# First projection of a two-layer diffusion backbone by halves of the features, and expert weights in longer DMA rows

## What is computed

```
def modulation(cond, w_mod, b_mod):
    m = jax.nn.silu(cond) @ w_mod + b_mod
    return jnp.split(m[..., None, :], 6, axis=-1)

def modulate(x, shift, scale):
    return x * (1.0 + scale) + shift
...
    z = h @ w_in                       # even layer: 1024 -> 1184, h = modulate(x, shift, scale)
...
def moe(h, router_w, router_bias, w_gate, w_up, w_down):
    ...
    hid = jax.nn.silu(jnp.einsum("nd,edf->nef", x, w_gate)) * jnp.einsum("nd,edf->nef", x, w_up)
    y = jnp.einsum("nef,efd->nd", hid * gates[:, :, None].astype(hid.dtype), w_down)
...
        xp = layer_norm(ALPHA * xp + mp[2] * op, ln_g[l, 0], ln_b[l, 0])
        hp = modulate(xp, mp[3], mp[4])
        fp = moe(hp, router_w, router_bias, exp_w_gate[l], exp_w_up[l], exp_w_down[l])
        xp = layer_norm(ALPHA * xp + mp[5] * fp, ln_g[l, 1], ln_b[l, 1])
```

## Time and profile before

| | us |
|---|---|
| median of 3 runs | 795.42 |
| the profiled execution, whole | 793.16 |
| its span, first to last instruction | 791.4 |
| PE busy | 734.0 (93%) |
| DVE, ACT, POOL busy | 237.2, 157.5, 73.1 |
| data moved | 287.40 MB, mean 363 GB/s |
| DMA packets | 67906, of them under 8 KB 51988 |

### The profile page before, as it was taken

The page is one execution under the profiler, slowest core; times in us unless marked ns, Lnnn a source line. Parts: engine busy times, 40 slices in busy tenths (PEclk is TensorE's granted clock), DMA queues, the critical chain, the costliest instruction groups (busy, mean ns, idle before and its releaser), DMA issues.

```text
span 791.4 us, 9516 instructions
## 1 busy us (share of the span) xinstructions
PE 734.0 (93%) x3745; PEld 345.0 (44%) x3745; DVE 237.2 (30%) x551; ACT 157.5 (20%) x408; POOL 73.1 (9%) x126
## 2 busy tenths in 40 slices
PE   4699899897999999998799999998999999998896
PEld 1345444455444443443234554454544434442432
DVE  0003544455310010100436228484501001000255
ACT  0201321325011110120103132343211101110201
POOL 0000000000200001102200110000200002101020
PEclk9899899997999999999999999999899999999998
DMA  8999999915499999999999999963299999999993
GB/s 324 397 322 410 410 409 419 417 77 213 186 420 416 417 422 415 421 416 416 419 399 379 409 410 418 397 239 144 98 420 416 422 418 416 422 416 419 415 409 116
DMA packets 67906, 287.40 MB, mean 363 GB/s; under 512 B 6636, under 2 KB 12268, under 8 KB 51988
## 3 DMA queue, kind: packets, MB, share of 16 engines
q1 hardware_dynamic: 63828, 275.54, 86.6%
q10 hardware_dynamic: 2880, 7.03, 2.2%
q0 software_dynamic: 1152, 4.19, 1.3%
HBM read 278.93 MB, written 7.82 MB: 362 GB/s over the span
## 4 chain that ended last, share of the span: by engine, by line
PE 51%; SPq 31%; DMA 9%; DVE 5%; ACT 2%; issue 2%; POOL 0%; DVEq 0%; ACTq 0%
PE bank L1171 14%; SPq L638 12%; PE bank L1207 7%; PE bank L987 7%; SPq L633 6%; DMA ring<-in_exp_w_up 6%; PE bank L838 5%; SPq L634 4%; PE bank L1138 4%; DMA ring<-in_w_mod 3%; PE bank L725 3%; SPq L598 3%; SPq L602 2%; PE bank L966 1%; PE bank L943 1%
## 5 line engine op out<-in xcount | busy, mean ns | idle before, releaser
L1171 PE MATMUL bank<-ring,arena 128*64 128x512 f32 x1024 | 226.2, 597 | 7.8 <-DMA ring<-in_exp_w_up 7.8
L1171 PEld LDWEIGHTS bank<-ring,arena 128*64 128x64 f32 x1024 | 73.5, 138 | 156.5 <-issue 151.5
L1207 PE MATMUL bank<-ring,arena 128*64 128x512 f32 x512 | 113.8, 595 | 6.8 <-DMA ring<-in_exp_w_down 5.7
L1787 DVE TENSOR_TENSOR arena<-bank,arena 128x256 f32<-128x256 f32 x32 | 13.6, 425 | 218.8 <-ACT arena L1993 218.5
L1207 PEld LDWEIGHTS bank<-ring,arena 128*64 128x64 f32 x512 | 36.3, 137 | 73.9 <-issue 66.0
L1138 PE MATMUL bank<-arena 128*128 128x128 f32 x512 | 63.5, 279 | 0.0
L1138 PEld LDWEIGHTS bank<-arena 128*128 128x128 f32 x512 | 61.1, 196 | 1.2 <-issue 0.7
L725 PE MATMUL bank<-ring,cwin 128*32 128x512 f32 x384 | 50.4, 665 | 11.0 <-DMA ring<-in_w_mod 10.4
L1884 ACT ACTIVATE arena<-bank 128x512 f32<-128x512 f32 (+5 forms) x65 | 34.8, 559 | 116.2 <-PE bank L838 32.6
L1993 ACT ACTIVATE arena<-bank 128x256 f32<-128x256 f32 x32 | 12.3, 383 | 219.2 <-PE bank L1171 219.2
L1803 DVE COPY arena<-bank 128x512 f32<-128x512 f32 x14 | 9.7, 691 | 121.9 <-PE bank L1207 121.9
(11 more groups left out here) (200 smaller groups left out, 652.7 us busy)
## 6 DMA issues: line engine op xcount, KB each, us to landing
ring<-in_exp_w_gate SPq DMA_DIRECT2D x62, 1024.0 KB, 20.6
ring<-in_exp_w_up SPq DMA_DIRECT2D x62, 1024.0 KB, 20.3
ring<-in_exp_w_down SPq DMA_DIRECT2D x60, 1024.0 KB, 22.5
ring<-in_w_mod SPq DMA_DIRECT2D x24, 2048.0 KB, 21.5
expert_rows<-arena ACTq DMA_DIRECT2D x12, 512.0 KB, 7.8
ring<-in_w_out_ab SPq DMA_DIRECT2D x2, 2048.0 KB, 23.6
ring<-in_exp_w_down SPq DMA_DIRECT2D x8, 512.0 KB, 15.0
ring<-in_w_in_c SPq DMA_DIRECT2D x2, 2048.0 KB, 18.0
```

What stands on the lines that cost most here:

```text
L1171: mm = nc.tensor.matmul(pb(key)[SLOTS * hf:SLOTS * (hf + 1), :], xeT[b][:, k * P + SLOTS * a:k * P + SLOTS * (a + 1)], w[:, :, k % 4, hf * ...
L1207: mm = nc.tensor.matmul(pb(key)[SLOTS * a:SLOTS * (a + 1), :], hp[:, c:c + SLOTS], w[:, a, kf % 2, hf * HALF:(hf + 1) * HALF], start=(kf = ...
```

## The change

1. `plan_blocks` and `load_block`: modulation pieces 0 to 3 become four blocks `top`, each with all eight k of 512 columns (rows of 2 KB where they had 4 KB). Pieces 0 and 2 hold the first half of the features of shift and scale, 1 and 3 the second. The three `win` blocks become ranges of k (0 to 2, 3 to 5, 6 and 7) with whole rows of 1184 columns. The order is top 0, top 2, win 0, top 1, top 3, win 1, win 2; x is loaded behind the second block.
2. On PE, `top_chunks(h)`, `even_rows_turned(h)` and `project_even(part)` take the place of `modulation(0, 0)`, `modulated(0, 0)` and `project(0)`: half of the columns, x of that half turned, three steps of k of the projection, then the other half. The six (column range, group) outputs stand open in banks 0 to 5 together. ACT and DVE make `hT` by halves.
3. `w_down` is laid out `(p k) c`: partition p holds four consecutive rows, so a block's two rows are one piece of 8 KB. Hidden value f then has to stand at partition f // 4, so `gate_up` reads the columns of gate and up with a step of four elements (16 bytes), in all pairs.
4. In pairs 1 to 6, where the two slots of an expert lie closer than 8 apart (`whole`), one slot holds the whole gate matrix and the other the whole up matrix, in pieces of 16 KB per partition. Each slot is loaded by two DMAs, partitions 0 to 63 and 64 to 127. `gate_up` waits for both slots before its first matmul and reads both at once. The first expert's two slots are released at the second matmul of the second expert, the second expert's first slot behind the gather (chunks 4 and 5), its other as before.

```
-    order = [("mod", 0, c) for c in MOD_PIECES[0]] + [("win", 0, b) for b in range(3)]
+    order = [("top", 0, 0), ("top", 0, 2), ("win", 0, 0), ("top", 0, 1), ("top", 0, 3), ("win", 0, 1), ("win", 0, 2)]
...
+        def whole(n):
+
+            l = order[n][1]
+            return exp_n[l] + 6 <= n < exp_n[l] + 6 * (N_PAIR - 1) and abs(slot[n] - slot[n + 1]) < RING - 2
+
+        def whole_pair(n):
+
+            a, b = slot[n], slot[n + 1]
+            both = ring.rearrange("p (s c) -> p s c", c=BLK)[:, min(a, b):max(a, b) + 1:abs(a - b), :]
+            return both.rearrange("p w (k m r) -> p w k r m", k=KD, r=4)
...
-        w_down = i_["exp_w_down"].rearrange("l e (k p) c -> (l e) p k c", p=P)
+        w_down = i_["exp_w_down"].rearrange("l e (p k) c -> (l e) p k c", p=P)
...
+                    elif t < 4 and whole(n + t - t % 2):
+                        m = n + t - t % 2
+                        src = (w_up if (t % 2 == 1) == (slot[m] < slot[m + 1]) else w_gate)[e + t // 2]
+                        for r in (0, 64):
+                            sp.dma_start(block_ap(n + t)[r:r + 64, :], src[r:r + 64, :]).then_inc(got(n + t)[0], 16)
...
-                        pe.wait_ge(*got(n + k // 4, i))
+                        if not whole(n):
+                            pe.wait_ge(*got(n + k // 4, i))
+                        elif k == 0:
+                            for m in range(2):
+                                pe.wait_ge(*got(n + m, i))
...
-                    w = block_ap(n + k // 4).rearrange("p (w k f) -> p w k f", w=2, k=4)
+                    if whole(n):
+                        w = whole_pair(n)[:, :, k]
+                    else:
+                        w = block_ap(n + k // 4).rearrange("p (w k m r) -> p w k r m", w=2, k=4, r=4)[:, :, k % 4]
...
-                                              w[:, :, k % 4, hf * 256:(hf + 1) * 256],
+                                              w[:, :, 2 * hf:2 * hf + 2, :],
...
+                        elif (k, hf) == (0, 1) and a == 1 and whole(n - 2):
+                            mm.then_inc(*release(n - 2))
...
-                    modulation(0, 0)
-                    pe.wait_ge(*saved(("mod", 0, 0)))
-                    mod_columns(0, 0)
-                modulated(l, 0)
-                if l == 0:
-                    project(0)
+                    top_chunks(0)
+                    even_rows_turned(0)
+                    project_even(0)
+                    top_chunks(1, index[("win", 0, 0)])
+                    even_rows_turned(1)
+                    project_even(1)
+                    project_even(2)
```

More of the change, by code:

```diff
@@ L211, in plan_turns @@
     t = Turns()
-    t.use(("mod", 0, 0), 7)
     t.use(("lnT",), 5)
-    t.use(("modT", 0, 0), 6)
+    for h in range(2):
+        t.use(("top", h), 7)
+        t.use(("topT", h), 6)
+        for g in range(G):
+            t.use(("hT", 0, 0, g, h), 6 + g if h else 2 * g)
     for l in range(DEPTH):
         for s in range(2):
-            for g in range(G):
-                for q in range(2):
-                    t.use(("hT", l, s, g, q), 2 * g + q)
+            if (l, s) != (0, 0):
+                for g in range(G):
+                    for q in range(2):
+                        t.use(("hT", l, s, g, q), 2 * g + q)
             if s == 0:
@@ L748, in modulation, with top_chunks @@
                                  start=False, stop=True, skip_group_check=True).then_inc(*fill(key))
+            def top_chunks(h, used=None):
+                key = ("top", h)
+                room(pe, key)
+                out = pb(key)
+                for c in (h, 2 + h):
+                    n = index[("top", 0, c)]
+                    pe.wait_ge(*got(n))
+                    w = block_ap(n).rearrange("p (k c) -> p k c", k=KD)
+                    for k in range(KD):
+                        j = k % 4
+                        mm = nc.tensor.matmul(out[32 * j:32 * j + 32, :], cwin[:, k, 24 - 2 * c:56 - 2 * c], w[:, k, :],
+                                              start=(c == h and k < 4), stop=False, skip_group_check=True)
+                        if (c, k) == (h, 0) and used is not None:
+                            mm.then_inc(*release(used))
+                    mm.then_inc(*release(n))
+                bias = tri[0:DEPTH * N_MOD, 0:1].to_broadcast([DEPTH * N_MOD, 32]) if h else \
+                    cst(C_BIAS, 32, DEPTH * N_MOD)
+                nc.tensor.matmul(out[0:32, :], bias, rows[0:DEPTH * N_MOD, :],
+                                 start=False, stop=True, skip_group_check=True).then_inc(*fill(key))
+                pe.wait_ge(*saved(key))
+                turn_rows(("topT", h), mods[0], C_SEL, 8)
             def turn_rows(key, src, c0, n):
@@ L824, in project_odd, with even_rows_turned @@
+            def even_rows_turned(h):
+                pe.wait_ge(s_x, 32)
+                for g in range(G):
+                    rows_turned(0, 0, g, h)
             def project_odd():
@@ L1176, in gate_up @@
                             mm.then_inc(*release(used))
-                        elif (k, hf) == (4, 0):
+                        elif (k, hf) == (0, 1) and a == 1 and whole(n - 2):
+                            mm.then_inc(*release(n - 2))
+                        elif (k, hf) == (4, 0) and not whole(n):
                             mm.then_inc(*release(n))
@@ L1230, in pair @@
                 room(pe, ("xe", l, 1), p + 1)
-                gather(pb(("xe", l, 1)), ahead, range(4, 6), P)
+                mm = gather(pb(("xe", l, 1)), ahead, range(4, 6), P)
+                if whole(n + 2):
+                    mm.then_inc(*release(n + 2))
                 room(pe, ("tp", l), p * 2 + 1)
@@ L1387, in _, with top_ab @@
             V = nc.vector
+            def top_ab(h):
+                key = ("topT", h)
+                shift, scale = (mod_cols(key)[:, a, :, h] for a in range(2))
+                a_, b_ = (ab[:, 0, a].rearrange("p g (h q) -> p g h q", h=2)[:, :, h] for a in range(2))
+                dve.wait_ge(*full(key))
+                V.tensor_scalar(a_, scale, 1.0, None, ALU.add)
+                V.tensor_copy(b_, shift).then_inc(*drain(key))
+                dve.wait_ge(*saved(key))
+                dve.sem_inc(s_ab2 if h else s_ab, 1)
             def mod_ab(l, s):
@@ L1395, in mod_ab @@
                 dve.wait_ge(*full(key))
[L1396 to L1408 removed]
+                dve.wait_ge(s_lnT, 1)
@@ L1409, in mod_ab, with modulated_columns @@
+                ch.then(V.tensor_scalar(sc, scale, 1.0, None, ALU.add))
+                for g in range(G):
+                    V.tensor_tensor(a_[:, g], sc[:, g], lnT[:, t - 1, 0], ALU.mult)
+                    last = V.tensor_tensor(b_[:, g], sc[:, g], lnT[:, t - 1, 1], ALU.mult)
+                ch.then(last)
+                V.tensor_tensor(b_, b_, shift, ALU.add).then_inc(*drain(key))
+                dve.wait_ge(*saved(key))
                 dve.sem_inc(s_ab, 1)
-            def modulated_columns(l, s):
+            def modulated_columns(l, s, q=1):
```

114 lines of the change are left out of this document (61 added, 53 removed).

## The result

The changed kernel takes 1057.24 us (median of 4 runs, 1054.61 to 1062.23), before takes 795.33 us (4 runs beside them): ratio 1.331, 95% interval 1.324 to 1.338. The forecast was 791 with a range to 890, so the result lies far outside it. The profiled execution took 1062.23 us with a span of 1060.3 us, 268.9 us more than before's 791.4.

What follows compares the result with a forecast made beforehand. The weight stream leads until 98.24 us, then PE until it catches up with the stream in the experts' pair 6. 793.16 - 6.7 (rows) + 3.4 (waiting) = 789.9, forecast 791 against before's median; range 782 to 890.

Steps and rivals of the forecast that it cites:

- rival 1: Experts' 16 KB slots: DMAs of 64 partitions run at down to half rate, up to +180 us, 967 us; chance 0.25.
- rival 2: Experts' gate and up: PE reading one value per 16 bytes takes up to twice the time, about 997 us; chance 0.10.
- It decides above 8%: Rival 2's threshold: PE's reserve against the stream is 7.6 us for 99 us of gate and up.
- The first projection: Start of the kernel: projection runs from near 24 to near 62.5 us, 6 us earlier, but counts 0.
- The cover: Attention still waits at 88.04 and 98.24 us for modulation blocks in the DMA stream, hiding the projection's 6 us.
- The rows of the experts: Experts' weight stream: longer rows save 6.7 us in both layers, bounds 0 and 7.5.
- The price of a piece: DMA stream: each piece costs 9.6 ns beside its bytes, so joining two saves 9.6 ns.
- Waiting for both slots: Pair 6 of each layer: PE idles about 4 us, then the lowered clock costs 1.7 us, 3.4 in all, bounds 0 and 7.
- Later releases: Pair 1's slots come free near 235.6 us, later than before, with 3 us of stream still queued; taken as 0.

Runs made afterwards that it cites:

- halves_only: The changed kernel with the step of four taken back, 16 KB slots still loaded in two halves of 64 partitions; 974.67 us, ratio 1.225.
- step alone: The changed kernel with each 16 KB slot loaded by one DMA of 128 partitions, the step of four kept; 1017.45 us, ratio 1.280.
- proj_only: The kernel before with only the first projection by feature halves added; 795.06 us, ratio 1.001.
- one_load: The changed kernel with the step of four taken back and each 16 KB slot loaded by one DMA of 128 partitions; 793.75 us, ratio 0.999.
- adj_whole5: adj_before plus whole 16 KB slots by one DMA in pairs 1 to 5 only and the first projection by feature halves; 790.86 us, ratio 0.996.
- adj_before: The kernel before with 8 KB down rows of two neighbouring features, so only the turning reads with step 2; 793.48 us, ratio 0.999.
- adj_one_load: adj_whole5 with whole 16 KB slots by one DMA in pair 6 too, so PE waits there for both slots; 792.18 us, ratio 0.997.
- clock_kept: adj_one_load with four dummy matmuls ahead of pair 6's wait for its second expert; 790.38 us, ratio 0.994.

## Why the prediction was wrong, step by step

**What failed.** Two steps were costed at nothing in the forecast and left to rivals 1 and 2: that the DMAs of 64 partitions keep the rate, and that PE keeps its pace on every fourth value. The runs showed half the rate (215 GB/s for 426) and 900 ns for 512 columns instead of 429. Both rivals came true at the upper end of their bounds: halves alone cost 181 us (bound 180), step alone 224 us (bound 204). The bound took twice the time for a pair; with the measured 15.07 us more, the prediction's own sum gives 8 x 15.07 - 7.6 = 113 a layer, 226. Either kernel alone, at 975 and 1017 us, lies outside the range to 890. The second failure is in the chances. They were 0.25 and 0.10, and they were treated as cases that exclude each other; nothing in the profile says so, for one concerns the DMA engines and the other PE. With both the range would have had to reach beyond 1000. For rival 1 the argument against was that engines may get out of step. Whether they do is not shown, but it brings nothing: 215 GB/s is half of 426. For rival 2 it was that PE asks for a value only every 0.84 ns. That holds, but 16 bytes cost 1.76 ns, and at step 4 each value lies in 16 bytes of its own.

**What held of the bounds.** "It decides above 8%" for the step was right, and the upper bound was a fair price. When a change makes every read of the largest group take a form for which the trace of before has no row, the bounds were there and the forecast stood at the favourable one.

**The first projection.** Worth 0, as forecast (proj_only), but not by its sum: it starts at 25.6 and ends at 69.8, not 24 and 62.5. PE of the changed kernel at the start:

```profile
25.61 14.71 PE L867 MATMUL bank<-ring,arena 128*128 128x416 f32 x36 [1.07 <-ACT arena L1988]
40.25 3.64 PE L790 MATMUL bank<-ring,cwin 128*32 128x512 f32 x32
...
48.39 21.45 PE L867 MATMUL bank<-ring,arena 128*128 128x416 f32 x60
69.77 7.08 PE L754 MATMUL bank<-ring,cwin 128*32 128x512 f32 x64
```
```profile
25.00:30.00 5.00, 4.39 (x7) 2.47 (x8) 0.95 (x3) 0.46 (x2) 0.00 (x0) 0.50 1.05 387
48.00:55.00 7.00, 7.00 (x19) 3.91 (x18) 1.37 (x4) 1.44 (x4) 0.00 (x0) 0.77 1.03 420
```

The start is 1.6 us late. The projection's two parts take 14.7 and 21.4 us for 12 and 20, because both begin behind stretches in which PE did little: the granted clock is 0.50 (1.2 GHz) in the first 5 us and 0.77 at the second start. Modulations and turning between them take 8.1 us for 6.6. So the projection ends about 1 us later than before and not 6 us earlier. The cover (the modulation blocks) was not put to the test; the modulation steps near 85 and 97 us end 0.8 and 0.3 us later than before.

**The rows of the experts.** The price of a piece was right: 611 ns for 16 KB by 9.6 ns beside the bytes, 612 measured in one_load. (Its sum has a slip: 4 KB at 410 GB/s are 159.8 ns and not 160.0, so it gives 9.2 ns and 10.3 as the bound for 9.6 and 10.8, and 6.4 us for 6.7.) The stretch reads 423 to 424 GB/s in adj_whole5, close to the forecast 424 to 427. Of the 3.1 us a layer that this kernel should save (2.0 for down and 0.15 for each of seven whole experts), 1.9 and 2.1 arrive; in adj_before it is 1.1 of 2.0. Why a third and more is missing stays open.

**Waiting for both slots.** The mechanism was right and so was its place: 3.9 us of idle time in pair 6 of both layers, with the clock down behind it. The term of 1.7 us a layer was met in two of four readings and too small in two: the 32 instructions take 8.78 and 10.04 us in one_load and 8.79 and 9.56 in adj_one_load for 7.09, so 1.7 to 3.0. In one_load it and the row saving nearly cancel: no difference from before.

**Later releases** at nothing: right for one_load, whose stretch 220 to 370 reads 421 GB/s (before has 418 there). In the changed kernel they are not nothing. PE holds each slot for longer, and from 210 to 300 the DMA share is 0.86: 12 us in which the slow stream stood still because SP waited for PE to release slots, and which it lacks later.

**A version that beats both**: clock_kept, 0.56% below before (interval 0.4 to 0.7%), and adj_whole5, 0.4%. Both are the idea of the change, longer rows, without its two faults.

## What to carry to other kernels

Before a layout is changed for longer DMA rows, look at what each reader of the new layout does with it: which partitions one DMA writes, and how many values a matmul takes from each 16 bytes. Where the trace of before has no row of that form and the group is the largest, the unfavourable bound is a forecast of its own, and two unknowns on different engines can both come true. A GB/s figure is read only together with the share beside it: 288 at 1.01 is a slow stream, 315 at 0.80 one that is not asked for more.

## What the runs showed of the hardware that was not expected

- PE's moving operand, read with a step of 16 bytes, costs about 1.76 ns a value (900 ns for 512 columns), alike for one full-width matmul and for two side by side; a step of 8 bytes costs only 6% more than a plain read.
- DMAs of 64 partitions run at full rate in partitions 32 to 95 (16 KB packets 611 ns) and at about half in 0 to 63 (1264 ns): it is the position, not the number.
- Three DMAs with the middle partitions first bring hardly any of the rate back (962 us, halves_only 975); why is open.
- An idle wait of 3.9 us costs 1.7 to 3.0 us once more in the work behind it; four dummy matmuls in the wait give it back in the traces.
